# A decoder layer on one core: tile 0's expert dots and gathers are started during its own search

## The reference

```python
def peer_block(xb, w_peer_q, sub_keys1, sub_keys2, peer_u, peer_v):
    q = (xb @ w_peer_q).reshape(n, PEER_HEADS, 2, PEER_QDIM // 2)
    s1 = jnp.einsum('nhd,kd->nhk', q[:, :, 0], sub_keys1)
    s2 = jnp.einsum('nhd,kd->nhk', q[:, :, 1], sub_keys2)
    v1, i1 = lax.top_k(s1, PEER_TOPK)
    v2, i2 = lax.top_k(s2, PEER_TOPK)
    cand = (v1[..., :, None] + v2[..., None, :]).reshape(n, PEER_HEADS, PEER_TOPK * PEER_TOPK)
    vs, ic = lax.top_k(cand, PEER_TOPK)
    experts = i1[ic // 16] * PEER_KEYS + i2[ic % 16]      # per head
    g = jax.nn.softmax(vs, axis=-1)
    act = jax.nn.gelu(jnp.einsum('nd,nhkd->nhk', xb, peer_u[experts]), approximate=False)
    return jnp.einsum('nhk,nhkd->nd', g * act, peer_v[experts])
```

## Time and profile before

| | |
|---|---|
| runs of the kernel | 3455.93, 3458.95, 3465.72 us; median 3458.95 us |
| span of the profiled execution | 3463.5 us |
| busy on PE, DVE, ACT, POOL | 2477.3, 2417.5, 448.7, 2050.1 us |
| bytes moved by DMA | 1321.82 MB, 382 GB/s over the span |
| gathers of `u` and of `v` | 1056 and 1056 |
| granted PE clock, mean of the span | 0.798 |

### The profile page before, as it was taken

One profiled execution on the slowest core, in us unless ns is written; L12 is line 12 of the kernel. 1 busy time (PEld: TensorE's weight loads), 2 busy tenths in 40 slices (PEclk: granted clock), 3 DMA queues, 4 the chain that ended last, 5 costly groups with the idle time before them and its releaser, 6 DMA issues.

```text
span 3463.5 us, 37116 instructions
## 1 busy us (share of the span) xinstructions
PE 2477.3 (72%) x11828; PEld 1269.7 (37%) x11828; DVE 2417.5 (70%) x7228; ACT 448.7 (13%) x992; POOL 2050.1 (59%) x2118
## 2 busy tenths in 40 slices
PE   6768665888756797696666667696766677667666
PEld 5644123653432344372332233372332233313200
DVE  4587757768778886867578865857568865957742
ACT  1101000113201231111000110112100110000000
POOL 0136754566646665547756775547756765576675
PEclk8878668898876788798877888898877788776667
DMA  6479999999999999999999999999999999999999
GB/s 257 169 262 396 372 342 398 378 382 355 388 407 383 382 357 389 411 382 409 410 411 410 404 409 411 397 366 406 410 410 410 406 405 407 392 408 411 382 408 373
DMA packets 373381, 1321.82 MB, mean 382 GB/s; under 512 B 60962, under 2 KB 72418, under 8 KB 352962
## 3 DMA queue, kind: packets, MB, share of 16 engines
q0 software_dynamic: 304128, 1107.43, 81.4%
q1 hardware_dynamic: 69058, 212.03, 15.8%
HBM read 1311.41 MB, written 7.88 MB: 381 GB/s over the span
## 4 chain that ended last, share of the span: by engine, by line
DMA 29%; PE 28%; DVE 21%; POOL 10%; issue 8%; SPq 2%; ACT 1%; DVEq 0%; POOLq 0%; ACTq 0%
DMA u_ring<-up_rows,codes 16%; DMA v_ring<-down_rows,codesT 9%; PE ps L905 7%; PE ps L968 7%; POOL v_ring L860 5%; POOL u_ring L847 5%; DMA wbuf<-weights 4%; DVE u_ring L1858 4%; DVE arena L1817 3%; PE ps L958 3%; DVE u_ring L1853 2%; PE ps L1175 2%; PE ps L1228 2%; DVE idx L1817 1%; DVE arena L1821 1%
## 5 line engine op out<-in xcount | busy, mean ns | idle before, releaser
L847 POOL DMA_INDIRECT u_ring<-up_rows,codes x1056 | 1023.4, 969 | 805.7 <-issue 262.6
L905 PE MATMUL ps<-v_ring,Z 128*32 128x512 f32 x4096 | 1058.2, 766 | 535.8 <-DMA v_ring<-down_rows,codesT 401.8
L860 POOL DMA_INDIRECT v_ring<-down_rows,codesT x1056 | 1025.5, 971 | 594.6 <-PE ps L905 317.4
L1853 DVE CUSTOM_DVE_ANT_0 u_ring<-u_ring,ps 128x1024 f32<-128x1024 f32 x577 | 690.6, 1217 | 405.9 <-DMA u_ring<-up_rows,codes 405.2
L1858 DVE CUSTOM_DVE_ANT_0 u_ring<-u_ring,xn 128x512 f32<-128x512 f32 x958 | 607.2, 686 | 107.3 <-DMA u_ring<-up_rows,codes 104.2
L905 PEld LDWEIGHTS ps<-v_ring,Z 128*32 128x32 f32 x4096 | 148.4, 122 | 1118.6 <-DMA v_ring<-down_rows,codesT 794.7
L1175 PEld LDWEIGHTS ps<-xT,wbuf 128*128 128x128 f32 x2176 | 311.9, 229 | 198.6 <-issue 119.1
L1175 PE MATMUL ps<-xT,wbuf 128*128 128x128 f32 (+1 forms) x2176 | 337.4, 318 | 58.8 <-DMA wbuf<-weights 58.5
L968 PE MATMUL ps<-wbuf,xT 128*128 128x256 f32 (+2 forms) x1184 | 290.2, 403 | 55.3 <-DMA wbuf<-weights 31.2
L968 PEld LDWEIGHTS ps<-wbuf,xT 128*128 128x128 f32 (+1 forms) x1184 | 228.4, 200 | 136.9 <-DMA wbuf<-weights 42.4
L1817 DVE MAX8 vals<-arena 128x8 f32<-128x128 f32 (+1 forms) x288 | 68.9, 280 | 87.9 <-ACT arena L1631 87.1
(11 more groups left out here) (341 smaller groups left out, 2564.6 us busy)
## 6 DMA issues: line engine op xcount, KB each, us to landing
wbuf<-weights SPq DMA_DIRECT2D x142, 1024.0 KB, 8.4
u_ring<-up_rows,codes POOLq DMA_INDIRECT x1056, 13.0
v_ring<-down_rows,codesT POOLq DMA_INDIRECT x1056, 12.6
u_ring<-weights SPq DMA_DIRECT2D x8, 1024.0 KB, 13.8
v_ring<-weights SPq DMA_DIRECT2D x8, 1024.0 KB, 14.0
wbuf<-weights SPq DMA_DIRECT2D x9, 768.0 KB, 8.4
resid<-x_prompt SPq DMA_DIRECT2D x8, 512.0 KB, 6.7
table<-decay_in SPq DMA_DIRECT2D x8, 512.0 KB, 10.1
```

The costliest lines, as they stand in the source:

```text
L847: pool.indirect_dma_start(out=u_ring[:, i % U_RING, :], out_offset=None, in_=up_rows, in_offset=bass.IndirectOffsetOnAxis(ap=codes[:, t % ...
L860: pool.indirect_dma_start(out=v_ring[:, v % V_RING, :], out_offset=None, in_=down_rows, in_offset=bass.IndirectOffsetOnAxis(ap=codesT[:, t ...
L905: mm = pe.matmul(acc[q:q + 32, half, :], (Zs if t == TILES else Z)[:, at:at + GS], v_ring[:, v % V_RING, half * 512:(half + 1) * 512], sta ...
L1853: ins = dve.tensor_tensor_reduce(u, u, x_spread if t == TILES else x_now, 1.0, 0.0, ALU.mult, ALU.add, dots[:, k:k + 1])
```

## The change

Tile 0 is no longer scheduled like the others. A list of its own, `FIRST_PEER`, puts 48 of its dots into its own search, the first 8 right behind the second head, and `FRONTS[1]` is made smaller, so that the front of tile 1 holds 65 slots in place of 95. From slot 113 on, which is the last `slots()` of the front of tile 1, the lists give the same numbers as before. These 48 dots read x from PSUM: `load_x(0, 1)` stands on ACT behind the copy of the transposed `xn`. Since group 0 (slots 0 to 31) is now weighted inside the search, the gates of heads 0 to 3 are asked for in step 4 and taken in step 5 (`FIRST_GATES`), those of heads 4 to 7 where all eight were before. And POOL issues nine of the `v` gathers among the first 32 `u` gathers.

```diff
+FIRST_GATES = 4
+def gate_heads(t, part):
+    return slice(0, H) if t else slice(part * FIRST_GATES, FIRST_GATES + part * (H - FIRST_GATES))
+def gate_no(t, part):
+    return t + 2 if t else 1 + part
...
-        FRONTS[1] = [3, 3, 4, 4, 4, 5] + [2] * 6 + [1] * H + [2, 2] + [4, 3, 4, 3, 4, 4, 4, 4, 3, 4] + [2, 2, 2, 2, 1, 2]
+        FRONTS[0] = [0] * len(FRONTS[0])
+        FRONTS[1] = [2, 2, 3, 3, 3, 3] + [1, 1, 2, 1, 1, 2] + [1, 0, 1, 1, 0, 1, 1, 0] + [1, 1] + [3, 2, 3, 2, 3, 3, 3, 2, 2, 3] + [1, 2, 1, 2, 1, 1]
...
         PEER = [[2, 2], [2, 2], [2, 1], [2, 2], [2, 2], [1, 2], [2, 2], [1, 2], [2, 2]]
-        TURN_OVER = 4
+        FIRST_PEER = [[0, 0], [0, 0], [0, 8], [4, 4], [4, 12], [3, 5], [3, 5], [0, 0], [0, 0]]
...
-            for t in range(1, TILES):
+            for t in range(TILES):
                 begin, end = X_RANGES[t]
-                if begin <= i < t * SLOTS:
-                    return 2 * t - 1
-                if t * SLOTS + 3 <= i < (end if t < TILES - 1 else TILES * SLOTS):
+                if t and begin <= i < t * SLOTS:
                     return 2 * t
+                if t * SLOTS + (3 if t else 0) <= i < (end if t < TILES - 1 else TILES * SLOTS):
+                    return 2 * t + 1
...
+            ahead = 0
             for k in range(GS):
                 u_rows(0, k)
+                if k >= GS - 2 * V_RING and k % 2:
+                    v_rows(0, 0, ahead)
+                    ahead += 1
...
             def load_x(t, of_own):
                 if of_own:
-                    act.wait_ge(dot_done, t * SLOTS)
+                    if t:
+                        act.wait_ge(dot_done, t * SLOTS)
                     act.wait_ge(wide_ready, wide_no(t, 2))
...
                 turned_copy(t, 2, n, None)
+                if t == 0:
+                    load_x(0, 1)
...
                     peer(t, s, n)
+                    if t == 0 and s == FIRST_GATES:
+                        gate_exps(0, n, 0)
                     slots()
...
+                    if t == 0 and s == FIRST_GATES + 1:
+                        take_gates(0, n, 0)
                     if 1 <= s <= here:
                         peer(t, s - 1, n, slots)
                     else:
                         slots()
+                    if t == 0 and s == FIRST_GATES:
+                        ask_gates(0, n, 0)
                     slots()
```

More of the change, by code:

```diff
@@ L869, in _ @@
                     for j in range(GS):
-                        v_rows(t, g, j)
+                        if (t, g) != (0, 0) or j >= ahead:
+                            v_rows(t, g, j)
                         if g + 1 < GROUPS:
@@ L1435, in load_x @@
                 src = xn[:, (t if of_own else t - 1) % 2].rearrange("p (a b) -> p a b", a=2)
-                own.raises(act.activation(x_now, src, ACT.Copy), x_loaded, 2 * t - 1 + of_own)
+                own.raises(act.activation(x_now, src, ACT.Copy), x_loaded, 2 * t + of_own)
             def groups(done, upto):
@@ L1632, in copy_keys, with gate_exps @@
                                keys_copied, H * t + h + 1)
-            def gate_exps(t, n):
-                act.wait_ge(gate_in, t + 1)
-                own.raises(act.activation(gate_x[0:n], gate_x[0:n], ACT.Exp), gate_exp, t + 1)
+            def gate_exps(t, n, part=1):
+                of = gate_heads(t, part)
+                act.wait_ge(gate_in, gate_no(t, part))
+                own.raises(act.activation(gate_x[0:n, of], gate_x[0:n, of], ACT.Exp), gate_exp, gate_no(t, part))
             def out_and_peer(t, n, slots, following):
@@ L2147, in gate_logits, with ask_gates, take_gates @@
                 take_gates(t, n)
-            def ask_gates(t, n):
-                do_signal(gate_in, t + 1, dve.tensor_tensor, gate_x[0:n], top_v[0:n],
-                          top_v[0:n, :, 0:1].to_broadcast([n, H, K]), ALU.subtract)
-            def take_gates(t, n):
-                dve.wait_ge(gate_exp, t + 1)
-                do(dve.tensor_reduce, ms8[0:n, 0:8], gate_x[0:n], AX_X, ALU.add)
-                do(dve.reciprocal, ms8[0:n, 0:8], ms8[0:n, 0:8])
-                do(dve.tensor_tensor, gates[0:n, t % 2].rearrange("p (h k) -> p h k", h=H), gate_x[0:n],
-                   over(ms8[0:n, 0:8], 2, [n, H, K]), ALU.mult)
+            def ask_gates(t, n, part=1):
+                of = gate_heads(t, part)
+                do_signal(gate_in, gate_no(t, part), dve.tensor_tensor, gate_x[0:n, of], top_v[0:n, of],
+                          top_v[0:n, of, 0:1].to_broadcast([n, of.stop - of.start, K]), ALU.subtract)
+            def take_gates(t, n, part=1):
+                of = gate_heads(t, part)
+                dve.wait_ge(gate_exp, gate_no(t, part))
+                do(dve.tensor_reduce, ms8[0:n, of], gate_x[0:n, of], AX_X, ALU.add)
+                do(dve.reciprocal, ms8[0:n, of], ms8[0:n, of])
+                do(dve.tensor_tensor, gates[0:n, t % 2].rearrange("p (h k) -> p h k", h=H)[:, of], gate_x[0:n, of],
+                   over(ms8[0:n, of], 2, [n, of.stop - of.start, K]), ALU.mult)
             HEADS_HERE = 6
```

14 lines of the change are left out of this document (6 added, 8 removed).

## The result

The changed kernel took 3472.55 us (median of 6 runs, 3465.26 to 3478.77); the kernel before took 3461.9 us beside it (median of 6, 3455.93 to 3465.72). The ratio is 1.0034, 95% interval 1.002 to 1.0048: slower, by little more than the 0.3% that the prediction could tell from nothing. In a second series, with new runs of both kernels, it was 1.0043, interval 1.0028 to 1.0058 (3470.87 against 3456.97 us). So the kernel is slower by some 11 to 15 us. Forecast were 3467 us and +7.5 us.

The account below looks back on a forecast made before the run. Work on DVE and PE, not the gathers, was taken to set the end of tile 1's front. 32.7 + 4.5 + 2 − 11 − 20.7 = +7.5 us on 3458.95 gave 3467 us, range 3444 to 3486.

Parts of the forecast that it names:

- Search, dots: Search of tile 0: 48 new dots from PSUM at 1.14 us replace 18 old ones, so DVE gets 32.7 us more.
- Search, the rest: Search of tile 0: small gate and coefficient instructions, waits for first `u` gathers, ScalarE's table load; +4.5 us, bounds 1.2 and 14.
- `load_x` and early V gathers: Search of tile 0: ACT's copy of x and nine early `v` gathers on POOL, both costed at nothing.
- Projection: Projection of tile 1, bounded by PE: `v` matmuls of 16 slots in place of 8; +2 us, bounds 0 and 5.
- Queries to attention: Tile 1's queries, retention and attention: 24 dots become 15, DVE leading; −11 us, bounds −5 and −16.
- Sample mixer: Tile 1's mixer: 33 dots ahead of the states become 23, `u` gather waits go, +2 lost cover; −20.7 us, bounds −10 and −25.
- the rival that the moved dots were cover: Front of tile 1: dots had filled DVE's waits for PE or ACT, 12 us of saving lost; +20 us, 3479 us; chance 0.24.
- the 3 us of new waits: Sign of the cover case: new DVE waits for PE or ACT of more than 3 us in attention or mixer.
- Output projection: Output projection after `store_states`: three dots fewer, worth nothing, since the wait for the third weight piece covers them.
- From there on the distance to every later landmark should be unchanged: Behind `store_states`, itself expected 5 to 12 us later: everything later just shifts.
- The rival with the gathers as pace: Front of tile 1: 20 slots fewer at 1.49 us per gather bring 59.5 us; −20 us, 3439 us; chance 0.17.
- a mixer of 90 us or less: Sign of the gather case: tile 1's sample mixer at 90 us or less, where the forecast had near 103 us.

## Why the prediction came out as it did

The direction was right and the total near, but the way there was not: +20.8 us stood at `store_states` where +7.5 was forecast, and the part behind it, costed at nothing, took back 6. That the total came so near is in part luck: the projection was costed 9 us too low and the attention gave back 5 us less than forecast, against 3 us more from the mixer and 6 us behind it.

- **Search, dots (+32.7): right.** The 48 dots cost what the rows said. Undoing their form moved the copy by 4.4 to 5.4 us against 3.8.
- **Search, the rest (+4.5): 6.2 by the copy, made up otherwise.** I had 2 us of waits for the first gathers; there were 1.1. I had not seen that V rows stand in TensorE's queue ahead of the last heads' products and the transposes: VectorE waited 3.57 us ahead of the copy at 246.98 us (2.12 in the second profile), and with 38 dots not at all.
- **`load_x` and early V gathers (0): wrong on what the gathers are for.** Without them the search is 7 to 8 us longer, so they don't cost, they pay. No run tests `load_x` by itself.
- **Projection (+2, bounds 0 to 5): the step that failed, +11.4.** I counted TensorE's own work and took the loads of the weight pieces to come in time as before; no term stood for the transfers that they would meet. TensorE is idle for 7.6 us more, and busy for 4.9 us more, of which 4.4 are the two pieces at the lower clock behind their waits. I had asked what the moved gathers do on GpSimd's queue, and not what they do to the loads on SyncE's. The moves of the state loads and the kernel with 38 dots each took back 9 to 10 us of it: it needs both the gathers at full pace and the state loads among the pieces.
- **Queries to attention (−11): −5.8,** between −2.1 and −9.4 by which profiles are paired; the attention of the kernel before varies by 5 us. The profile that I had read was the longer of the two here. VectorE has 8 dots fewer, 14 in place of 22.
- **Sample mixer (−20.7): −23.8.** It has 11 dots fewer by count, 24 in place of 35, or 13.4 us, and the waits for `u` gathers, 10.5 and 9.7 us in the two profiles, are gone. VectorE's waits for TensorE in the mixer grew from 8.8 us to 13.0 and 11.1 in the two profiles, and one of 2.0 us for ScalarE went. That is 0.3 to 2.2 us of lost cover, where I had put in 2, and far from the 12 of the rival, so the rival that the moved dots were cover falls, though the first profile passes the 3 us of new waits that I had named as its sign. The two longest stand in its list of waits, 395.5 to 483.9 us; the second was 0.2 us before, and the first 8.6:

```profile
DVE kT L1844 <- PE ps L1366: 8.2, 4, 2.1
DVE vN L1844 <- PE ps L1353: 3.0, 2, 1.9
```

- **Output projection (0, covered by the wait for the third weight piece): −6.1, and −8.2 behind it.** The slots were hidden on VectorE, but they were not free. The run with 11 slots in this place shows 9.4 of the 14 us. That it is their gathers, which run beside that piece, is likely and not shown.
- **"From there on the distance to every later landmark should be unchanged": wrong.** Besides the above, the stretch with the search of tile 2 and the front of tile 3 took 6.7 us longer in the mean. One program gave 413.2 and 406.6 us there in two executions, the other 406.5 and 399.9, and all fourteen profiles lie between 399.9 and 413.2. The three with the old lists have 399.9, 403.4 and 406.5; of the eleven others eight are longer than all three. So the change may have a part in it, but with so few I can't tell. The lists give the same slots at the same places there: the 4 in place of 3 at the head of tile 3's front only makes up for another way of counting. No run tested it.

The rival with the gathers as pace was wrong in its time. Its sign, a mixer of 90 us or less, did not show either: that was said of the stretch from 354.5 to 478.7 us before (VectorE's copy of the turned input ends it), and the same stretch lasts 99.6 and 98.0 us now, near the 103 of the forecast. The 88 us of the table end at `store_states`. The DMA share, forecast to be well under 0.9, is 0.88 in the attention and 0.83 in that stretch of the first profile. What the rival had right is that gathers can be dear where a weight piece is awaited beside them.

## What to carry to other kernels

When work with transfers is moved, list for its new place every transfer that is awaited there, on every queue, and what stands ahead of it: here 1 MB was there after 8 us or after 19.5, by whether small loads stood in front of it on its queue while the gathers ran at full pace. A load that nobody needs soon belongs behind the last one that somebody does, and not just ahead of it, as the two moves with 38 dots show (ratios 1.0058 and 1.0026). Take a second profile of the kernel before you price a stretch: one of mine was 5 us off its repeat in a stretch of 61 to 66.

## What was new of the hardware

Eight DMA issues of 32 KB on SyncE took 3.8 to 5 us while the DMA engines kept up, and 12.8 and 12.9 us in the two profiles at a DMA share of 1.04. So here the full DMA engines show on the issuing queue as long issues. During one of these, from 264 to 270 us, the two queues were served 615 packets each, so that the one with small packets moved 0.14 MB beside 2.24 MB of the other; in the second profile it was 619 to 620 (265 to 271 us). And behind tile 4's input, at 1342 to 1369 us, all fourteen profiles take 2110.3 to 2115.8 us to the end, though their spans differ by 27 us: what tells these executions apart, of one kernel or of two, arises before it. Between two executions of one program it was the attention of tile 1 and the stretch up to tile 4's input.
